# Differential attention and a gated recurrence on one core: heads unrolled, weighting in one fp32 product, factors of q on GpSimd

## The chip, the core and the metric

The program runs on one core of a Trainium2 chip. The time is the device time of one execution in microseconds; the median of three runs counts. The profile comes from a single execution recorded by the hardware profiler. TensorE is called PE there, its weight load PEld, VectorE is DVE, ScalarE is ACT, GpSimd is POOL and the queue of SyncE, which issues the DMAs, is SP. "PEclk" is the clock granted to TensorE as a share of 2.4 GHz; it has the two levels 0.50 (1.2 GHz) and 1.00.

## What is computed

One layer over 2048 tokens of width 1024, all in float32. One projection gives queries, keys and values of a differential attention (4 heads, two softmax maps of 64 features each, values of 128) and q, f, i and gate of a recurrence (HGRN2, 4 heads of 128). Both results go through one output projection, and a gated feed-forward part follows. What the change touches is this:

```python
# attention, for each block of 128 queries; mask: key chunk <= query chunk (chunks of 64)
s = jnp.einsum('bhqd,bhkd->bhqk', q_blk, k)
p = jax.nn.softmax(jnp.where(mask, s, -jnp.inf), axis=-1).reshape(B, H, 2, Q_BLOCK, S)
w = p[:, :, 0] - lam * p[:, :, 1]
out = jnp.einsum('bhqk,bhkv->bhqv', w, v)          # then RMS norm per head
# recurrence: S_t = diag(f_t) S_{t-1} + k_t v_t^T,  o_t = S_t^T q_t,  k_t = 1 - f_t
# then orr = rms_norm(o) * silu(gate)
```

## The kernel before

The program has three stages, one after the other, each a block of five engine programs that meet by semaphores: `project`, `mix_tokens` and `feed`. TensorE multiplies in fp32r. Where full precision is wanted, an operand is split into a high part in fp32r and the low rest, and three products (high x high, high x low, low x high) are added up.

`project` goes through 4 blocks of 512 tokens in 14 units of 256 columns. Of the units V (4 and 5) ScalarE writes the high part (L329) and VectorE the low part (L410); both are stored to `v_hi` and `v_lo` (L208).

`mix_tokens` runs a hardware loop over the 4 heads (`Fori`), on each engine (L778, L825, L889, L1022, L1140). Beside head h of attention it runs block h of the recurrence, all four of its heads at once. The body has 16 unrolled steps j, one for each block of 128 queries, and a seventeenth for what is left.

- A step scores both maps m against (j + 1) x 128 keys (`score`, L1066 to L1070) into a ring of four PSUM banks, in runs of up to two banks. VectorE takes the maximum of each run (`maximum`, L928, and over the runs L933). ScalarE takes the exponential and its sum (`exponentiate`, L851), which frees the banks. VectorE then forms inverse sums and the difference of both maps in one pass over the keys (`combine`, L948 to L957).
- One step later the weights are turned by TensorE in groups of four tiles (`turn`, L1081) into one of two PSUM banks. ScalarE writes their high part (`group_high`, L861), VectorE the low part (`group_low`, L963), and TensorE multiplies three times per tile with v (`weigh`, L1093 to L1095). There are 136 tiles per head. ScalarE reads the output and its squares (`read_output`, L866 and L870).
- The recurrence is spread over the steps as "fills", two in each of the first 15 steps, through one PSUM bank `fill_bank`: four diagonals (L1107), 14 level products (7 levels x 2 sides, L1117), four transposes of k, then output and state by turns (L1131 to L1136). A fill may start when the one before it has been read. After the fill of a level, VectorE multiplies q with a factor (`raise_level`, L970; at the diagonals L985) and only then copies the fill under a mask (L992). GpSimd meanwhile multiplies k (L839). The next level of that side waits for both. GpSimd also forms the factors (L832) and multiplies the output with the gate (L844).
- At the end of a head, outside the steps, come square roots, reciprocals and 16 scalings (L1051) of the output, then eight chunks of four transposes each (L1178) with a copy by ScalarE (L916, L918) and the stores of `mix`. Before the loop turns, SP has issued the loads of k, v and q for the next head (L793 to L807); k and v have a single buffer.

`feed` does the output projection and the feed-forward part. All its products have 512 columns.

Of the kernel before, what the change touches and what calls it, by code (L numbers as in the profile page):

```python
# [16 lines left out]
P = 128  # L17
D = 1024
SEQ = 2048
# [100 lines left out]
def project(nc, x, attn_g, w_in, q_g, k_g, ident, pair_sel, eps, out, masks):  # L120
# [15 lines left out]
    with ExitStack() as ctx:  # L136
# [66 lines left out]
        def destinations(u, tok):  # L203
# [3 lines left out]
            if u in V:  # L207
                return [token_dst(out[k], V[0], u, tok) for k in ("v_hi", "v_lo")]  # L208
# [65 lines left out]
        HANDED = [(u, t) for u in (*V, *HQ, *HG) for t in range(UT)]  # L274
# [6 lines left out]
        def _(act):  # L281
# [24 lines left out]
            def finish(i, n):  # L306
# [20 lines left out]
                for t in range(UT):  # L327
                    if u in V:
                        nc.scalar.activation(first[:, t, :].bitcast(F32R), banks[t][:], ACT.Copy).then_inc(act_part, 1)  # L329
                    elif u in HQ or u in HG:  # L330
                        nc.scalar.activation(second[:, t, :], banks[t][:], ACT.Sigmoid).then_inc(act_part, 1)
                    elif u in HI:
# [4 lines left out]
                if u in HI or u in HF:  # L337
                    last.then_inc(finished[par].sem, 1)
# [23 lines left out]
        def _(dve):  # L362
# [20 lines left out]
            def finish(i, n):  # L383
# [140 lines left out]
def mix_tokens(nc, mid, lambdas, subln_g, hgrn_g, ident, eps, mask, mix):  # L524

# [36 lines left out]
    GATE_STEP = len(FILLS) // 2  # L562
    assert HEADS == BLOCKS and GATE_STEP < SEQ // P
    STEPS = SEQ // P
    RING = 4
    RUN_BANKS = 2
    GROUP = 512 // P
    MASKED = -1e30

    def banks_of(j):  # L570

        return j // GROUP + 1
# [3 lines left out]
    for j in range(STEPS):  # L576
        for m in range(2):
            runs[j, m], key, left = [], 0, (j + 1) * P
            while left:
                n = min(RING - at, RUN_BANKS, -(-left // 512))  # L580
                width = min(left, n * 512)
                runs[j, m].append((at, key, width))
                at, key, left = (at + n) % RING, key + width, left - width
    assert at == 0
    order = [(j, m, r) for j in range(STEPS) for m in range(2) for r in range(len(runs[j, m]))]
    RUNS = len(order)
    MAX_RUNS = max(len(rs) for rs in runs.values())
    RUN_AT = {key: n for n, key in enumerate(order)}

    freed, last_in = {}, {}  # L590
    for n, (j, m, r) in enumerate(order):
        bank, _, width = runs[j, m][r]
        mine = range(bank, bank + -(-width // 512))
        freed[j, m, r] = max([last_in.get(x, -1) for x in mine]) + 1
        last_in.update({x: n for x in mine})
    GROUPS = sum(banks_of(j) for j in range(STEPS))
    GROUP_AT = {(j, g): sum(banks_of(i) for i in range(j)) + g for j in range(STEPS) for g in range(banks_of(j))}
    assert GROUPS % 2 == 0

    def tiles_in(j, g):  # L600

        return min(GROUP, j + 1 - g * GROUP)

    with ExitStack() as ctx:
        a = Alloc(nc, ctx, "att")


        q_hl = [a.sb(f"q_hl{b}", [P, 2, TB], F32R) for b in range(2)]
        q_lh = [a.sb(f"q_lh{b}", [P, 2, TB], F32R) for b in range(2)]
        k_hl = a.sb("k_hl", [P, 2, SEQ], F32R)  # L610
        v_hi = a.sb("v_hi", [P, STEPS, P], F32R)
        v_lo = a.sb("v_lo", [P, STEPS, P], F32R)
# [14 lines left out]
        wt_hi = [a.sb(f"wt_hi{b}", [P, 512], F32R) for b in range(2)]  # L627
        wt_lo = [a.sb(f"wt_lo{b}", [P, 512], F32R) for b in range(2)]
        o_all = a.sb("o_all", [P, STEPS, P])
# [4 lines left out]
        o_turned = a.sb("o_turned", [P, SEQ])  # L634
# [7 lines left out]

# [10 lines left out]
        ro_turned = r.sb("o_turned", [P, HEADS, TB])  # L653
        fill_bank = r.bank("fill")

        waited = a.sem("waited")
# [4 lines left out]
        k_in = [a.sem(f"k_in{b}") for b in range(2)]  # L661
# [10 lines left out]
        group_turned = a.sem("group_turned")  # L672
        group_hi = a.sem("group_hi")
        group_lo = a.sem("group_lo")
# [6 lines left out]
        o_turn_done = a.sem("o_turn_done")  # L681
        o_staged = a.sem("o_staged")
# [991 lines left out]
```

## Time and profile before

| | us |
|---|---|
| median of 3 runs | 3421.8 |
| lowest, highest | 3421.25, 3426.63 |
| span of the profiled execution | 3422.3 |
| TensorE busy | 3191.2 (93%) |
| VectorE busy | 1561.6 (46%) |
| ScalarE busy | 1158.8 (34%) |
| GpSimd busy | 143.5 (4%) |

The busy times are sums over the whole span. The ends of matmuls are modelled and each overlaps the next one, so a product's cost is read from the distance between two starts. The three stages lie at about 0 to 749, 749 to 1691 and 1691 to 3422 us.

### The profile page before, as it was taken

To read this page: it belongs to the slowest core of one execution; us is meant where nothing else is said; L and a number is where in the kernel's file an instruction comes from. 1 tells how busy PE (TensorE), PEld (TensorE's weight loads), DVE (VectorE), ACT (ScalarE), POOL (GpSimd) and SP (SyncE) were. 2 spreads that over 40 slices of the span, in tenths; PEclk is the share of its full clock that TensorE was granted. 3 is DMA by queue.
4 is the path that set the end of the run, shared out by engine and by line. 5 is a ranking of instruction groups with operands and counts; after the bars stand their busy time and mean duration, and the time that the engine had idled before them with its cause. 6 is when DMAs were issued, how large, how long until landed. Compare 5 with 4: busy or idle time off the path is not lost.

```text
span 3422.3 us, 44330 instructions
## 1 busy us (share of the span) xinstructions
PE 3191.2 (93%) x16832; PEld 2767.6 (81%) x16832; DVE 1561.6 (46%) x2066; ACT 1158.8 (34%) x1713; POOL 143.5 (4%) x122
## 2 busy tenths in 40 slices
PE   6999999979878888888699999999999999999999
PEld 5898989868778778777588887888878888788887
DVE  3434243426747657667435533355333543334432
ACT  3333333322523424424333322333223332233322
POOL 3000000002011101110000000000000000000000
PEclk9999999986957858769699999999999999999999
DMA  3545454554141231321632234323342333433334
GB/s 126 170 151 181 141 169 143 189 173 113 26 123 38 66 108 38 87 65 35 191 103 91 95 111 130 97 94 98 105 135 93 98 98 102 136 95 98 98 98 129
DMA packets 337554, 379.45 MB, mean 111 GB/s; under 512 B 11760, under 2 KB 286704, under 8 KB 337392
## 3 DMA queue, kind: packets, MB, share of 16 engines
q1 hardware_dynamic: 337392, 377.14, 35.6%
q8 instruction: 120, 1.97, 0.2%
q14 instruction: 42, 0.34, 0.0%
HBM read 314.19 MB, written 62.91 MB: 110 GB/s over the span
## 4 chain that ended last, share of the span: by engine, by line
PE 47%; DMA 1%; issue 1%; ACT 1%; SPq 0%; DVE 0%; DVEq 0%; ACTq 0%
PE feed_prod L1514 15%; PE feed_prod L1516 15%; PE feed_prod L1515 15%; DMA feed_gate_work<-mix 1%; PE feed_prod L1577 1%; PE feed_sums L1530 1%; PE feed_turned L1543 0%; ACT feed_ff_hi L1381 0%; DMA feed_w_raw<-in_w_out_dram 0%; SPq L1305 0%; ACT feed_ff_work L1281 0%; SPq L1293 0%; PE feed_scales L1591 0%; SPq L1269 0%; DVE feed_ff_lo L1443 0%
## 5 line engine op out<-in xcount | busy, mean ns | idle before, releaser
L1514 PE MATMUL feed_prod<-feed_h_hi,feed_w_hi 128*128 128x512 f32 x1408 | 548.9, 390 | 0.0
L1516 PE MATMUL feed_prod<-feed_h_hi,feed_w_lo 128*128 128x512 f32 x1408 | 547.8, 389 | 0.0
L1515 PE MATMUL feed_prod<-feed_h_lo,feed_w_hi 128*128 128x512 f32 x1408 | 547.8, 389 | 0.0
L1438 DVE TENSOR_TENSOR feed_w_lo<-feed_w_raw,feed_w_hi 128x2048 fp32r<-128x2048 f32 (+1 forms) x152 | 339.6, 2234 | 383.7 <-ACT feed_w_hi L1373 383.7
L1514 PE MATMUL feed_prod<-feed_ff_hi,feed_w_hi 128*128 128x512 f32 x960 | 381.6, 398 | 32.3 <-DVE feed_ff_lo L1443 22.4
L1373 ACT ACTIVATE feed_w_hi<-feed_w_raw 128x2048 fp32r<-128x2048 f32 (+1 forms) x152 | 283.4, 1865 | 356.6 <-PE feed_prod L1516 317.6
L1515 PE MATMUL feed_prod<-feed_ff_lo,feed_w_hi 128*128 128x512 f32 x960 | 377.1, 393 | 0.0
L1516 PE MATMUL feed_prod<-feed_ff_hi,feed_w_lo 128*128 128x512 f32 x960 | 376.9, 393 | 0.0
L851 ACT ACTIVATE att_expo<-att_ring,att_neg_max 128x1024 f32<-128x1024 f32 (+4 forms) x192 | 165.2, 864 | 434.7 <-DVE att_neg_max L928 234.7
L1516 PEld LDWEIGHTS feed_prod<-feed_h_hi,feed_w_lo 128*128 128x128 f32 x1408 | 264.3, 188 | 55.2
L1515 PEld LDWEIGHTS feed_prod<-feed_h_lo,feed_w_hi 128*128 128x128 f32 x1408 | 264.4, 188 | 54.8
L1514 PEld LDWEIGHTS feed_prod<-feed_h_hi,feed_w_hi 128*128 128x128 f32 x1408 | 264.4, 188 | 54.0
L1514 PEld LDWEIGHTS feed_prod<-feed_ff_hi,feed_w_hi 128*128 128x128 f32 x960 | 182.6, 190 | 69.9 <-DVE feed_ff_lo L1443 22.6
L506 PE MATMUL proj_prod<-proj_w_hi,proj_h_hi 128*128 128x256 f32 x768 | 219.3, 286 | 0.0
L367 DVE TENSOR_TENSOR proj_w_lo<-proj_w_raw,proj_w_hi 128x2048 fp32r<-128x2048 f32 x57 | 130.5, 2290 | 190.3 <-ACT proj_w_hi L288 190.3
L507 PE MATMUL proj_prod<-proj_w_lo,proj_h_hi 128*128 128x256 f32 x768 | 217.2, 283 | 0.0
L508 PE MATMUL proj_prod<-proj_w_hi,proj_h_lo 128*128 128x256 f32 x768 | 217.2, 283 | 0.0
L1516 PEld LDWEIGHTS feed_prod<-feed_ff_hi,feed_w_lo 128*128 128x128 f32 x960 | 182.3, 190 | 38.5
L1515 PEld LDWEIGHTS feed_prod<-feed_ff_lo,feed_w_hi 128*128 128x128 f32 x960 | 182.8, 190 | 36.7
L516 PE MATMUL proj_prod<-proj_h_hi,proj_w_hi 128*128 128x512 f32 x512 | 204.4, 399 | 7.7 <-DVE proj_w_lo L367 5.9
L1093 PE MATMUL att_out<-att_v_hi,att_wt_hi 128*128 128x128 f32 x544 | 183.3, 337 | 25.6 <-DVE att_wt_lo L963 24.7
L518 PE MATMUL proj_prod<-proj_h_hi,proj_w_lo 128*128 128x512 f32 x512 | 200.6, 392 | 0.0
(171 smaller groups left out, 5310.7 us busy)
## 6 DMA issues: line engine op xcount, KB each, us to landing
proj_w_raw<-in_w_in_dram SPq DMA_DIRECT2D x58, 1024.0 KB, 7.1
feed_w_raw<-in_w_gate_dram SPq DMA_DIRECT2D x44, 1024.0 KB, 5.4
feed_w_raw<-in_w_up_dram SPq DMA_DIRECT2D x44, 1024.0 KB, 5.4
feed_w_raw<-in_w_down_dram SPq DMA_DIRECT2D x32, 1024.0 KB, 5.9
feed_w_raw<-in_w_out_dram SPq DMA_DIRECT2D x18, 1024.0 KB, 6.7
feed_w_raw<-in_w_down_dram SPq DMA_DIRECT2D x16, 768.0 KB, 4.5
proj_x_tok<-in_x_dram SPq DMA_DIRECT2D x5, 2048.0 KB, 12.8
feed_x_piece<-in_x_dram SPq DMA_DIRECT2D x17, 512.0 KB, 4.2
```

The costliest lines, as they stand in the source:

```text
L506: pe.matmul(dst, hi[:, s, tok], wh[:, s, :], start=s == 0, stop=False)
L507: pe.matmul(dst, hi[:, s, tok], wl[:, s, :], start=False, stop=False)
L508: last = pe.matmul(dst, lo[:, s, tok], wh[:, s, :], start=False, stop=s == KS - 1)
L516: pe.matmul(dst, wh[:, s, col], hi[:, s, :], start=s == 0, stop=False)
L518: last = pe.matmul(dst, wl[:, s, col], hi[:, s, :], start=False, stop=s == KS - 1)
L851: nc.scalar.activation(expo[j % 2][:, m, key:key + width], ring[:, bank * 512:bank * 512 + width], ACT.Exp, bias=neg_max[:, j % 2, m:m + 1 ...
L1093: pe.matmul(out_bank[:, 0:P], hi, v_hi[:, kt, :], start=kt == 0, stop=False)
L1373: nc.scalar.activation(w_hi[slot][:, 0:slabs, :], w_raw[slot][:, 0:slabs, :], ACT.Copy).then_inc(w_hi_made, 1)
L1438: nc.vector.tensor_tensor(w_lo[slot][:, 0:slabs, :], w_raw[slot][:, 0:slabs, :], w_hi[slot][:, 0:slabs, :].bitcast(F32), ALU.subtract).the ...
L1514: pe.matmul(dst, w_hi[slot][:, k, col], hi[:, s, :], start=first, stop=False)
L1515: pe.matmul(dst, w_hi[slot][:, k, col], lo[:, s, :], start=False, stop=False)
L1516: return pe.matmul(dst, w_lo[slot][:, k, col], hi[:, s, :], start=False, stop=stop)
```

## The change

The hardware loop over the heads is gone. All engines run through one sequence of 64 steps s (and two more), so that a step may hold score work of one head and turning, weighting and reading of the head before. Buffers that a head had alone are doubled: the first 512 keys (`k_first`), `v` and `o_all`.

v stays one fp32 array. ScalarE copies the turned weights in fp32 into one of four buffers (`take_group`), and `weigh` makes one fp32 product per tile. `group_low` goes. The weighting of groups 2 and 3 of a step moves behind the first scores of the step after the next.

GpSimd now multiplies q as well, right behind k on each side and level, and at the diagonals. VectorE keeps the masked copy. The two sums of `combine` become one instruction. VectorE's order in a step is the first maximum, then `combine` of the step before.

The end of a head moves into the next one: roots in its step 1, scaling (`normalise`, one instruction for 16) in step 2, and two chunks in each of steps 3 to 6 through three staging buffers, each stored when it is made. The last head's end stays behind its last step. SP's order of loads and stores changes with it.

Core of the diff:

```diff
-                return [token_dst(out[k], V[0], u, tok) for k in ("v_hi", "v_lo")]
+                return [token_dst(out["v"], V[0], u, tok)]
...
-                    if u in V:
-                        nc.scalar.activation(first[:, t, :].bitcast(F32R), banks[t][:], ACT.Copy).then_inc(act_part, 1)
-                    elif u in HQ or u in HG:
+                    if u in HQ or u in HG:
                         nc.scalar.activation(second[:, t, :], banks[t][:], ACT.Sigmoid).then_inc(act_part, 1)
...
-                elif u in V:
-                    for t in range(UT):
-                        dve.wait_ge(act_part, handed(i, n, t))
-                        last = nc.vector.tensor_tensor(second[:, t, :].bitcast(F32R), banks[t][:], first[:, t, :], ALU.subtract)
...
+    def chunks_at(s):
+        h, j = divmod(s, STEPS)
+        if s == TOTAL + 1:
+            return [(HEADS - 1, c) for c in range(CHUNKS)]
+        first = 2 * (j - FIRST_CHUNK_STEP)
+        if 0 < h < HEADS and 0 <= first < CHUNKS:
+            return [(h - 1, first), (h - 1, first + 1)]
+        return []
...
-        wt_lo = [a.sb(f"wt_lo{b}", [P, 512], F32R) for b in range(2)]
-        o_all = a.sb("o_all", [P, STEPS, P])
+        wt = [a.sb(f"wt{b}", [P, 512]) for b in range(WT)]
+        o_all = [a.sb(f"o_all{b}", [P, STEPS, P]) for b in range(2)]
...
+            def store(h, c):
+                n = h * CHUNKS + c
+                sp.wait_ge(staged, n + 1)
+                if c < TURNS:
+                    dst = mix[h * P:(h + 1) * P, c * 512:(c + 1) * 512]
+                else:
+                    dst = mix[W + (c - TURNS) * P:W + (c - TURNS + 1) * P, h * TB:(h + 1) * TB]
+                sp.dma_start(dst, stage[n % STAGES][:]).then_inc(stored[n % STAGES], 16)
...
+                    if h:
+                        step_scored(h - 1, STEPS - 1)
+                    load_first_k(h + 1)
+                    if h:
+                        sp.wait_ge(group_used, WEIGH[h * STEPS - 1, groups_of(h * STEPS - 1) - 1] + 1)
+                    load_v(h + 1)
+                    sp.wait_ge(q_ready[1], h * UPDATES + 2)
+                    load_features(rf, "hf", h + 1, rf_in)
                 step_scored(h, GROUP - 1)
                 load_q(h, 2)
+                if h:
+                    for c in range(CHUNKS):
+                        store(h - 1, c)
+                    sp.wait_ge(r_gated, h)
...
+                    sp.wait_ge(fill_done, filled(h, fill_at("k", 1, CH - 1)))
+                    load_features(rk, "hk", h + 1, rqk_in)
+                    step_scored(h, 3 * GROUP - 1)
+                    load_q(h + 1, 0)
+                    sp.wait_ge(fill_done, filled(h, len(FILLS) - 1))
+                    load_features(rq, "hq", h + 1, rqk_in)
+                    load_tokens(rv, "hv", h + 1, rv_in)
+                    step_scored(h, STEPS - 1)
+                    load_rest_k(h + 1)
...
+                for side in range(2):
+                    pool.wait_ge(fill_done, filled(h, fill_at("diagonal", side, HALF - 1)))
+                    nc.gpsimd.tensor_tensor(half(rq, side), half(rq, side), half(rf, side), ALU.mult).then_inc(q_ready[side], 1)
...
-                fill_read.wait(pool, filled(h, len(FILLS) - 1))
+                        pool.wait_ge(q_ready[side], h * UPDATES + m + 1)
+                        nc.gpsimd.tensor_tensor(runs_of(rq, side, m, 1), runs_of(rq, side, m, 1), factor(side, m, 1), ALU.mult).then_inc(q_ready[side], 1)
...
+            def take_group(s, g):
+                k, n = WEIGH[s, g], tiles_in(s, g) * P
+                slot = SLOT["w", s, g]
+                act.wait_ge(slot_turned, slot + 1)
+                if k >= WT:
+                    act.wait_ge(group_used, k - WT + 1)
+                nc.scalar.activation(wt[k % WT][:, 0:n], turned[slot % 2][:, 0:n], ACT.Copy).then_inc(slot_taken, 1)
+            def take_chunk(h, c):
+                slot, n = SLOT["f", h, c], h * CHUNKS + c
+                act.wait_ge(slot_turned, slot + 1)
+                if n >= STAGES:
+                    act.wait_ge(stored[n % STAGES], 16 * (n // STAGES))
+                col = g_col if c < TURNS else rg_col
+                nc.scalar.activation(stage[n % STAGES][:], turned[slot % 2][:], ACT.Copy, scale=col[:]).then_inc(slot_taken, 1)
+                act.wait_ge(slot_taken, slot + 1)
+                act.sem_inc(staged, 1)
...
+            for s in range(TOTAL + 2):
+                h, j = divmod(s, STEPS)
+                live = s < TOTAL
+                groups = range(groups_of(s - 1)) if 1 <= s <= TOTAL else ()
+                if live:
+                    exponentiate(s, 0)
+                if s >= 2 and groups_of(s - 2) > 2:
+                    read_output(s - 2)
+                if j == 1 and h:
+                    take_roots(h - 1)
+                if live and j < FILL_STEPS:
+                    read_fill(h, 2 * j)
+                for g in groups[:2]:
+                    take_group(s - 1, g)
+                if live:
+                    exponentiate(s, 1)
+                    if j < FILL_STEPS:
                         read_fill(h, 2 * j + 1)
...
+                for g in groups[2:]:
+                    take_group(s - 1, g)
+                if 0 < len(groups) <= 2:
+                    read_output(s - 1)
+                for head, c in chunks_at(s):
+                    take_chunk(head, c)
...
-            def group_low(h, j, g):
-                k, n = GROUP_AT[j, g], tiles_in(j, g) * P
-                dve.wait_ge(group_hi, h * GROUPS + k + 1)
-                nc.vector.tensor_tensor(wt_lo[k % 2][:, 0:n], turned[k % 2][:, 0:n], wt_hi[k % 2][:, 0:n].bitcast(F32), ALU.subtract).then_inc(group_lo, 1)
...
-            def raise_level(h, side, m):
-                if m:
-                    dve.wait_ge(whole_made, h * LEVELS + m)
-                dve.wait_ge(q_ready[side], h * UPDATES + m + 1)
-                nc.vector.tensor_tensor(runs_of(rq, side, m, 1), runs_of(rq, side, m, 1), factor(side, m, 1), ALU.mult).then_inc(q_ready[side], 1)
...
+            def normalise(h):
+                dve.wait_ge(r_rms_made, h + 1)
+                nc.vector.reciprocal(ro_rrms[:], ro_rms[:]).then_inc(r_rrms_made, 1)
+                dve.wait_ge(o_rms_made, h + 1)
+                nc.vector.reciprocal(o_rrms[:], o_rms[:]).then_inc(o_rrms_made, 1)
+                dve.wait_ge(o_rrms_made, h + 1)
+                o = o_all[h % 2][:]
+                nc.vector.tensor_tensor(o, o, o_rrms[:].unsqueeze(2).to_broadcast([P, STEPS, P]), ALU.mult).then_inc(o_normed, 1)
+                dve.wait_ge(r_rrms_made, h + 1)
+                dve.wait_ge(r_gated, h + 1)
+                out = ro[:].rearrange("p c (h n) -> p (c h) n", n=C)
+                nc.vector.tensor_tensor(out, out, ro_rrms[:].unsqueeze(2).to_broadcast([P, CH * HEADS, C]), ALU.mult).then_inc(r_scaled, 1)
...
+            for s in range(TOTAL + 2):
+                h, j = divmod(s, STEPS)
+                live = s < TOTAL
+                fills = live and j < FILL_STEPS
+                if live:
+                    maximum(s, 0)
+                if 1 <= s <= TOTAL:
+                    combine(s - 1)
+                if fills:
+                    read_fill(h, 2 * j)
+                if live:
+                    maximum(s, 1)
+                if fills:
+                    read_fill(h, 2 * j + 1)
+                if live and h and j == FIRST_CHUNK_STEP - 1 or s == TOTAL + 1:
+                    normalise(h - 1)
...
+            def weigh(s, g):
+                h, j = divmod(s, STEPS)
+                pe.wait_ge(slot_taken, SLOT["w", s, g] + 1)
+                if g == 0 and s:
+                    pe.wait_ge(o_read, s)
+                    pe.wait_ge(o_squared, s)
+                for t in range(tiles_in(s, g)):
...
-                    hi, lo = wt_hi[k % 2][:, t * P:(t + 1) * P], wt_lo[k % 2][:, t * P:(t + 1) * P]
-                    pe.matmul(out_bank[:, 0:P], hi, v_hi[:, kt, :], start=kt == 0, stop=False)
-                    pe.matmul(out_bank[:, 0:P], hi, v_lo[:, kt, :], start=False, stop=False)
-                    last = pe.matmul(out_bank[:, 0:P], lo, v_hi[:, kt, :], start=False, stop=kt == j)
+                    last = pe.matmul(out_bank[:, 0:P], wt[WEIGH[s, g] % WT][:, t * P:(t + 1) * P], v[h % 2][:, kt, :], start=kt == 0, stop=kt == j)
...
+            def turn_chunk(h, c):
+                slot = SLOT["f", h, c]
+                if c < TURNS:
+                    pe.wait_ge(o_normed, h + 1)
+                else:
+                    pe.wait_ge(r_scaled, h + 1)
+                open_slot(slot)
+                for t in range(GROUP):
+                    src = o_all[h % 2][:, c * GROUP + t, :] if c < TURNS else ro[:, t, (c - TURNS) * C:(c - TURNS + 1) * C]
+                    last = pe.transpose(turned[slot % 2][:, t * P:(t + 1) * P], src, ident[:])
+                last.then_inc(slot_turned, 1)
...
+                    score(s, 0)
+                if s >= 2:
+                    for g in range(2, groups_of(s - 2)):
+                        weigh(s - 2, g)
+                if fills:
+                    if j == 0:
+                        pe.wait_ge(rqk_in, 32 * (h + 1))
+                    fill(h, 2 * j)
+                if live:
+                    score(s, 1)
+                for g in groups[:2]:
+                    turn(s - 1, g)
+                if fills:
+                    fill(h, 2 * j + 1)
+                if j == 1 and live:
+                    pe.wait_ge(v_in[h % 2], 16 * (h // 2 + 1))
+                for g in groups:
+                    if g < 2:
+                        weigh(s - 1, g)
+                    if g + 2 in groups:
+                        turn(s - 1, g + 2)
+                for head, c in chunks_at(s):
+                    turn_chunk(head, c)
```

## Rows read from the trace of the kernel before

**Rows 1.** Stages and low-clock stretches: us, busy (instructions), PEclk, DMA share, GB/s.
```profile
761.00:1691.00 930.00, 784.84 (x4544) 711.81 (x4544) 587.51 (x1035) 353.64 (x833) 110.40 (x88) 0.75 0.29 79
1720.00:3422.00 1702.00, 1681.70 (x7705) 1400.37 (x7703) 681.53 (x683) 529.53 (x523) 0.00 (x0) 0.99 0.34 106
949.00:993.00 44.00, 36.50 (x157) 33.15 (x157) 19.72 (x39) 16.48 (x33) 3.21 (x6) 0.50 0.47 110
997.00:1062.00 65.00, 55.64 (x236) 51.70 (x236) 35.46 (x61) 12.77 (x40) 9.51 (x7) 0.50 0.22 72
```

**Rows 2.** The same view, pieces of 3 us at the second head's end.
```profile
1178.00:1181.00 3.00, 1.12 (x6) 0.68 (x4) 3.00 (x1) 0.00 (x0) 2.92 (x2) 1.00 0.16 53
...
1193.00:1196.00 3.00, 3.00 (x17) 3.00 (x16) 0.11 (x1) 0.77 (x3) 0.00 (x0) 0.50 0.99 231
```

**Rows 3.** Timeline of weight loads: start us, us, engine, line, out<-in, count.
```profile
937.83 0.97 PEld L1136 LDWEIGHTS rec_fill<-rec_v,rec_k_tok 128*128 128x128 f32 x8 [0.88 <-ACT rec_o L885]
...
939.70 0.19 PEld L1093 LDWEIGHTS att_out<-att_v_hi,att_wt_hi 128*128 128x128 f32 x1
939.82 0.19 PEld L1094 LDWEIGHTS att_out<-att_v_lo,att_wt_hi 128*128 128x128 f32 x1
...
963.36 0.33 PEld L1093 LDWEIGHTS att_out<-att_v_hi,att_wt_hi 128*128 128x128 f32 x1
963.57 0.33 PEld L1094 LDWEIGHTS att_out<-att_v_lo,att_wt_hi 128*128 128x128 f32 x1
...
1004.99 1.78 PEld L1107 LDWEIGHTS rec_fill<-rec_q,rec_k 128*128 128x128 f32 x8 [0.56 <-DVE rec_score L981]
```

**Rows 4.** Groups of TensorE: busy us, mean ns, idle before.
```profile
L1094 PEld LDWEIGHTS att_out<-att_v_lo,att_wt_hi 128*128 128x128 f32 x544 | 133.1, 245 | 0.0
...
L1136 PE MATMUL rec_fill<-rec_v,rec_k_tok 128*128 128x128 f32 x128 | 18.5, 288 | 10.7 <-ACT rec_o L885 10.7
```

**Rows 5.** Timeline across the first head's end, TensorE.
```profile
984.53 0.41 PE L1095 MATMUL att_out<-att_v_hi,att_wt_lo 128*128 128x128 f32 x1
...
1001.38 0.47 PE L1066 MATMUL att_ring<-att_k_hl,att_q_hl 128*128 128x128 f32 x1 [6.69 <-issue]
```

**Rows 6.** Waits, attention stage: in total, times, longest us.
```profile
ACT att_expo L851 <- DVE att_neg_max L928: 234.7, 63, 8.6
...
PE att_out L1093 <- DVE att_wt_lo L963: 24.7, 32, 2.1
PE rec_fill L1117 <- DVE rec_score L992: 23.9, 20, 2.7
PE att_ring L1066 <- ACT att_expo L851: 23.3, 23, 2.6
```

**Rows 7.** Groups by shape of VectorE and GpSimd: busy us, mean ns.
```profile
L970 DVE TENSOR_TENSOR rec_q<-rec_q,rec_whole 128x512 f32<-128x512 f32 x48 | 74.0, 1541 | 56.5 <-PE rec_fill L1117 55.2 <-issue 0.9
L957 DVE SCALAR_TENSOR_TENSOR att_expo<-att_expo,att_ratio 128x1920 f32<-128x1920 f32 x4 | 13.9, 3476 | 0.1
L957 DVE SCALAR_TENSOR_TENSOR att_expo<-att_expo,att_ratio 128x2048 f32<-128x2048 f32 x4 | 9.4, 2352 | 0.1
...
L839 POOL TENSOR_TENSOR rec_k<-rec_k,rec_whole 128x512 f32<-128x512 f32 x48 | 53.8, 1122 | 210.0 <-PE rec_fill L1117 210.0
L844 POOL TENSOR_TENSOR rec_o<-rec_o,rec_gate 128x2048 f32<-128x2048 f32 x4 | 18.3, 4577 | 318.8 <-DVE rec_state L997 318.8
```

**Rows 8.** DMA issues: count, KB each, median us to landing.
```profile
mix<-att_o_turned SPq DMA_DIRECT2D x16, 256.0 KB, 6.3
```

**Rows 9.** Timeline of step 14 and the next step's start.
```profile
929.80 0.45 PE L1066 MATMUL att_ring<-att_k_hl,att_q_hl 128*128 128x512 f32 x1
...
931.34 2.21 DVE L928 TENSOR_REDUCE att_run_neg_max<-att_ring 128x1 f32<-128x1024 f32 x2
...
933.78 1.11 ACT L851 ACTIVATE att_expo<-att_ring,att_neg_max 128x1024 f32<-128x1024 f32 x1 [5.38 <-DVE att_neg_max L933]
...
944.87 0.45 PE L1066 MATMUL att_ring<-att_k_hl,att_q_hl 128*128 128x512 f32 x1
```

More of the change, by code:

```diff
@@ L591, in mix_tokens @@
[L591 to L602, printed above, removed]
+    RUN_AT = {}
@@ new lines, in mix_tokens @@
+    for s in range(TOTAL):
+        for m in range(2):
+            for r in range(len(runs[s, m])):
+                RUN_AT[s, m, r] = len(RUN_AT)
+    freed, last_in = {}, {}
+    for (s, m, r), n in RUN_AT.items():
+        bank, _, width = runs[s, m][r]
+        mine = range(bank, bank + -(-width // 512))
+        freed[s, m, r] = max([last_in.get(x, -1) for x in mine]) + 1
+        last_in.update({x: n for x in mine})
+    MAX_RUNS = max(len(rs) for rs in runs.values())
+    assert all(len(runs[s, 0]) == len(runs[s, 1]) for s in range(TOTAL))
@@ new lines, in runs_through, with partial_runs @@
+    def runs_through(s, m):
+        return RUN_AT[s, m, len(runs[s, m]) - 1] + 1
+    def partial_runs(s, m):
+        return sum(len(runs[key]) for key in runs if key <= (s, m) and len(runs[key]) > 1)
+    def chunks_at(s):
[6 more added lines that the diff above has]
+        return []
@@ new lines, in load_rest_k, with load_v, load_features @@
+            def load_rest_k(h):
+                for part, name in ((low, "qk_hi"), (high, "qk_lo")):
+                    sp.dma_start(k_rest[part].bitcast(F32), rows(name, h, W, slice(TB, SEQ))).then_inc(k_rest_in, 16)
+            def load_v(h):
+                src = mid["v"][:, h * P:(h + 1) * P].rearrange("(t p) n -> p t n", p=P)
+                sp.dma_start(v[h % 2][:], src).then_inc(v_in[h % 2], 16)
+            def load_features(tile, name, b, sem):
+                sp.dma_start(tile[:], mid[name][:, b * TB:(b + 1) * TB].rearrange("(h p) n -> p h n", p=P)).then_inc(sem, 16)
@@ new lines, in _ @@
+            load_rest_k(0)
+            load_q(0, 1)
+            load_tokens(rv, "hv", 0, rv_in)
+            load_tokens(rgate, "hgate", 0, rgate_in)
+            for h in range(HEADS):
+                last = h == HEADS - 1
+                if not last:
+                    if h:
[6 more added lines that the diff above has]
+                    load_features(rf, "hf", h + 1, rf_in)
@@ L823, in _ @@
+            for c in range(CHUNKS):
+                store(HEADS - 1, c)
+            for b in range(STAGES):
+                sp.wait_ge(stored[b], 16 * len(range(b, HEADS * CHUNKS, STAGES)))
         @block.gpsimd
         def _(pool):
-            with pool.Fori(0, HEADS) as h:
-                pool.wait_ge(r_in, h * (16 * R_DMAS) + 16 * R_DMAS)
+            for h in range(HEADS):
+                pool.wait_ge(rf_in, 16 * (h + 1))
                 for m in range(LEVELS):
```

425 lines of the change are left out of this document (141 added, 284 removed).

## The prediction

> **What bounds the kernel now.** I first read the kernel by its three stages. The middle one, attention with its recurrence, takes 930 us of 3422; the stage after it holds TensorE busy 1682 of 1702 us at the full clock, and the change does not touch it [rows 1]. In the middle stage TensorE is busy 785 us (84%), VectorE 588, ScalarE 354 and GpSimd 110, and the granted clock is 0.75 [rows 1]. So TensorE bounds this stage too, but at a clock that is only at times the full one.
>
> Next I cut one head, 1002 to 1233 us, into 3 us pieces. TensorE is at 1.2 GHz (0.50) for the first 60 us, at 2.4 GHz in the middle, and at 1.2 GHz again over the head's end; [rows 1] has both low stretches for the turn from the first to the second head. The fall at the end comes right behind a piece in which TensorE is busy 1.12 of 3 us. Then it stays low for 40 us though a piece such as 1193 to 1196 is full to the brim [rows 2]. That piece holds little but products of 128 columns.
>
> Then I looked at pitches, from start to start, because a matmul's duration in the trace overlaps the next one. In the weighting of the values (L1093 to L1095) one fp32r product of 128 columns follows the other in 0.21 us at the low clock and in 0.11 us at the full one [rows 3]. An fp32 product shows as two records: 64 products of L1136 stand as 128 [rows 4]. The weight loads give the pitch of these records: eight of L1107 span 1.78 us at the low clock, less one of 0.33 over seven steps, 0.207 us; eight of L1136 span 0.97 at the full clock, less 0.19, 0.111 us [rows 3]. So one fp32 record costs the same pitch as one fp32r product.
>
> Last come the waits and the head's end. From the last weighting (984.53) to the next head's first score (1001.38) lie 16.8 us, of which 6.69 stand under "issue", at the jump back of the loop [rows 5]. Inside the head TensorE waits for VectorE's low part (L963), for L992 and for the exponentials L851 [rows 6].
>
> **The change part by part.**
>
> *One fp32 product for three fp32r ones.* 544 tiles give up three pitches and take two. Which clock they see follows from the mean weight load of L1094, 245 ns [rows 4]: with 0.19 us at the full clock and 0.33 at the low one [rows 3], 38% run low. The mean pitch is 0.62 x 0.111 + 0.38 x 0.213 = 0.150 us, and 544 x 0.150 = 81 us of TensorE's path go. The nearest rows for the new cost are L1131 and L1136, which are fp32 with 128 columns as well; the whole 1.78 us of L1107 over eight instead of seven pitches give 0.222 [rows 3], 0.009 more for 1088 records, which would leave 71 us, the lower bound; the upper one is 81, since no row has a cheaper record.
>
> The Trainium skill says in "FP8 and Floating Point Precision" (TensorE Precision Notes) that true fp32 makes 4 passes through the array. If a pass cost what an fp32r product costs here, the change would add a pitch per tile and lose 81 us where I book a gain. The trace shows two records at one pitch each, so I give that outcome a small chance as a rival below.
>
> *The low part on VectorE goes* (L963). VectorE has slack, so the time itself is worth nothing; the wait of TensorE for it, 24.7 us [rows 6], goes. What is late next is ScalarE's copy, which stood ahead of L963 anyway. The weighting of groups 2 and 3 moves one step later with four weight buffers, which covers this copy too.
>
> *q's factors move to GpSimd.* The 48 L970 of levels 1 to 6 take 74 us from VectorE [rows 7]; eight of level 0 and eight wide L985 I put at a quarter of that, 20. On GpSimd the 48 cost what k's do, 1.12 us [rows 7], 54, and the sixteen others at most two of these each, 36: GpSimd comes to 110 + 90 = 200 of 930 us, no bound. On VectorE they stood between a fill and its copy L992, and TensorE's single fill bank waits for that copy: 23.9 us [rows 6]. An L970 of 1.54 us goes from a chain of about 2.5, so I book 60%, 14 us. New is a serial chain on GpSimd: k, then q, 2.3 us per side and level, before the next level of that side. What hides it is the step between them, 10 us and more; without that cover it costs 56 x 2.3 us. GpSimd's work also slows VectorE's: the 1920-wide L957, which falls beside L844 in three heads of four, took 3.48 us on average against 2.35 for one of 2048 [rows 7], half of itself more. The L957 of steps 2 to 8 are short, some 7 us per head together by their widths, so this costs between 0 and 4 x 3.5 = 14 us; I take 0, because VectorE is not the bound there.
>
> The Trainium skill's "GPSIMD Engine Reference" (4.1 Engine selection) would keep an elementwise product of tensors on VectorE, since GpSimd takes about twice as long. It speaks against this part. The rows have k's on GpSimd at 1.12 us and q's on VectorE at 1.54, when both run at once.
>
> *Heads unrolled and spread ends.* The 16.8 us hold 32 transposes of 0.213 us, 6.8 us, which stay but go into steps 3 to 6 of the next head. The other 10 us, three times, go: 30 us [rows 5]. The code without a loop has no jump back; the trace shows "issue" waits of this kind only at the returns. I take 0 for fetching straight code, with one 6.69 us wait per head, 27 us, as the upper bound. Behind SP's waits for stores stand the loads of q 3 and k; their consumers are four steps away. The last head still ends alone, now through three staging buffers for eight chunks. A store lands in 6.3 us [rows 8] and two rounds wait for it, partly behind the work: 8 us lost, between 0 and 13.
>
> *v in one array* takes 16 VectorE operations and half the stores from the first stage, which TensorE bounds: 0.
>
> *The clock.* The fall at 1181 comes behind a wait for VectorE's L957, slowed by GpSimd, with the turns and the weighting behind it. In the new order the next score and the deferred weighting lie in between, so I expect the stretch to stay at the full clock. From 949 to 993 TensorE is busy 36.5 us at the low clock [rows 1]; less 31 tiles x 0.213 = 6.6 already booked, half of the remaining 30 us is 15, of which I book 14 per head: 56. A short dip of 10 us per head (near 881 and 1113) is worth some 3 us: 12. The low start of a head, 65 us [rows 1], should end about one step sooner, since less work of 128 columns stands in it: 5 per head, 20. Less 4 for tiles counted low in the first part. Sum 84; bounds 0 and about 165 (the start of each head warm too: 55.6 us busy, half of it 28, less what is booked).
>
> **The sum.** 81 + 25 + 14 + 30 + 84 - 8 = 226 us. Against the profiled run's span of 3422.3, which lies 0.5 us over the median of 3421.8, that gives 3196. A second way: step 14 now takes from 929.80 to 944.87 [rows 9]. Its chain afterwards is twice (one score pair 0.93, two maxima 2.21, 0.15 for the smaller, an exponential of 1.11 and 0.2 for its sum) = 9.2 us [rows 9] plus some 1.8 for state and fill, so 11 in place of 15. Six such steps at 3.5, step 15 with its weighting (40 us, to 984.53) down to some 23, and the first eight steps with 36 tiles x 0.213 and a quarter of the fill bank's 14 are 49 us per head; four of these, the 30 of the head ends and the 20 of the sooner full clock are 246, less 8 for the end: 238, or 3184. I forecast between the two: **3190 us**.
>
> **The rivals.**
>
> *A: the clock stays as it is now.* For it: TensorE full of 128-column work stayed low from 1193 to 1196 [rows 2]. Then only 81 + 25 + 14 + 30 - 8 = 142 us go: 3280. Chance 0.22.
>
> *B: TensorE is warm nearly throughout.* For it: the falls come behind waits, the stage after it, with hardly a wait, stays at the full clock for 1702 us [rows 1], and the new order takes most waits away. Then all 165 of the clock: 3115, and with shorter waits some 3095. Chance 0.18.
>
> *C: an fp32 product costs four pitches.* 544 x 0.150 more instead of less: 3190 + 163 = 3353. Against it stand the two records of L1136 [rows 4]. Chance 0.02.
>
> *D, slower than before: GpSimd's chain becomes the bound.* In steps 2 to 8 of each head four of its operations stand in a row per step. At 1.12 us each they take 4.5 us against steps of 10 to 14. If each cost what the contended L844 does, 4.58 us [rows 7], a step would take 18.3 + 3 us, about 11.7 more, in 28 steps: 3190 + 328 = 3518. It decides from about 4.1 us more per fill, that is, over 3 us per operation, where L839 has 1.12 [rows 7]. Chance 0.03.
>
> *E: the change doesn't do what it says.* A load or a code fetch that comes late leaves the heads unjoined: 30 + 27 us back, 3247. Chance 0.06.
>
> **How the numbers follow.** The forecast has 0.49. A lies at the upper side and B at the lower, so the range for 8 in 10 reaches from 3090 to 3290. A change under 0.2% (7 us) could not be told from none. Only C and D lie far off, and only D is slower: faster 0.95, same 0.01, slower 0.04.
>
> **What the new profile would show.** Two records per tile at 0.11 or 0.21 us in the weighting; VectorE some 200 us less busy in the stage and GpSimd at about 190; no "issue" wait of 6.7 us between heads; scores of a new head among the weighting of the last; granted clock of the stage over 0.80. The stage should last about 700 us. It would be wrong if TensorE waited for rec_q on GpSimd, if the clock stayed at 0.75 or less, or if ScalarE's exponentials, which now wait 235 us for VectorE's maxima [rows 6], became a chain that leaves TensorE idle for long.

## The result: 3134.5 us, 290 us less than before

| | before | after |
|---|---|---|
| median of the runs | 3424.2 us | 3134.5 us |
| span of the profiled execution | 3422.3 us | 3133.0 us |
| mean granted clock of TensorE | 0.925 | 0.979 |

The ratio is 0.915, with a 95% interval of 0.913 to 0.917. The before of this table has one run more than the three shown ahead, which puts its median 2.4 us higher. The gain is 290 us; the forecast had 232. The range (3090 to 3290) holds the time, but the time lies nearer to rival B (20 us away) than to the forecast (56 us).

### The profile page after: what moved, and what is told of

Same layout as the page of the kernel before. It is cut to its first block, busy times and chain, and to the rows that moved or that the text cites. A ratio compares the mean times of both kernels' runs of the same rounds, so it can differ in the third digit from the quotient of the medians.

```text
span 3133.0 us, 40790 instructions
## 1 busy us (share of the span) xinstructions
PE 2956.9 (94%) x16288; PEld 2561.2 (82%) x16288; DVE 1381.6 (44%) x1702; ACT 1156.5 (37%) x1712; POOL 248.7 (8%) x186
## 4 chain that ended last, share of the span: by engine, by line
PE 52%; DMA 1%; issue 1%; ACT 1%; SPq 0%; DVE 0%; DVEq 0%; ACTq 0%
PE feed_prod L1476 17%; PE feed_prod L1478 16%; PE feed_prod L1477 16%; DMA feed_gate_work<-mix 1%; PE feed_prod L1539 1%; PE feed_sums L1492 1%; PE feed_turned L1505 0%; ACT feed_ff_hi L1343 0%; DMA feed_w_raw<-in_w_out_dram 0%; SPq L1267 0%; ACT feed_ff_work L1243 0%; SPq L1255 0%; PE feed_scales L1553 0%; SPq L1231 0%; DVE feed_w_lo L1412 0%
## 5 line engine op out<-in xcount | busy, mean ns | idle before, releaser
L511 PE MATMUL proj_prod<-proj_h_lo,proj_w_hi 128*128 128x512 f32 x512 | 200.0, 391 | 0.0
```

What stands on the lines that cost most here:

```text
L511: pe.matmul(dst, wh[:, s, col], lo[:, s, :], start=False, stop=False)
```

## The profile after

First the page's busy times, then the windows view (us; busy and instructions of PE, PEld, DVE, ACT, POOL; PEclk; DMA share; GB/s) of the time from attention's first score to TensorE's end, of before and after, and of the attention stage after:

```profile
PE 2956.9 (94%) x16288; PEld 2561.2 (82%) x16288; DVE 1381.6 (44%) x1702; ACT 1156.5 (37%) x1712; POOL 248.7 (8%) x186
```
```profile
761.10:3418.00 2656.90, 2482.66 (x12320) 2125.66 (x12319) 1278.22 (x1724) 893.55 (x1366) 110.40 (x88) 0.91 0.32 97
```
```profile
762.40:3129.00 2366.60, 2248.34 (x11776) 1919.25 (x11775) 1108.30 (x1376) 891.88 (x1365) 215.66 (x152) 0.98 0.34 102
762.40:1410.00 647.60, 550.82 (x4000) 505.78 (x3999) 419.70 (x688) 355.54 (x835) 215.66 (x152) 0.93 0.35 93
935.00:949.00 14.00, 9.54 (x43) 8.95 (x43) 7.43 (x10) 4.19 (x10) 6.25 (x4) 0.51 0.64 175
```

Before and after differ by 544 TensorE records, one per tile. The attention stage lasts 648 us at a clock of 0.93, where [rows 1] has 930 us at 0.75. In each of heads 1 to 3 one wide stretch is left at the low clock, for instance 935 to 949, and one dip of 3.4 us. The first head still starts low, until 781, and the last one ends low.

The gain can be split by a bookkeeping that adds up by its making. From the first score to the end, the time is TensorE's idle time, plus its busy time; and its busy time is counted as its work at the full clock plus half of what it was busy at the low clock. It says how large each part is, not what caused it. All runs of this study are split in the same way here, each from its one profiled execution (us, worked out from TensorE's records merged and the stretches of the granted clock; the last column is the median of the timed runs; an execution that is profiled can lie some us off it, up to 7 here):

| kernel | time to the end | idle | busy at low clock | work at full clock | median |
|---|---|---|---|---|---|
| before | 2656.8 | 174.1 | 408.2 | 2278.6 | 3424 |
| + fp32 product alone | 2538.9 | 192.3 | 242.1 | 2225.5 | 3303.8 |
| + loop written out alone | 2630.8 | 155.5 | 391.5 | 2279.6 | 3398.0 |
| + q's factors on GpSimd alone | 2605.7 | 156.1 | 343.8 | 2277.7 | 3367.4 |
| + these three | 2432.7 | 146.9 | 120.5 | 2225.5 | 3197.2 |
| after (the change) | 2366.2 | 117.9 | 68.1 | 2214.3 | 3134.5 |
| after, q's factors on VectorE | 2445.2 | 129.6 | 202.3 | 2214.4 | 3206.7 |
| after, two fp32r products | 2374.6 | 117.6 | 92.2 | 2210.8 | 3143.2 |
| after, three fp32r products | 2413.9 | 102.1 | 86.7 | 2268.5 | 3189.0 |
| after, one fp32r product | 2332.2 | 125.8 | 104.9 | 2154.0 | 3101.2 |
| after, no deferral | 2408.3 | 141.8 | 94.0 | 2219.5 | 3177.4 |
| after, scalings in pieces | 2367.7 | 114.4 | 77.4 | 2214.6 | 3136.9 |
| after, scalings on ScalarE | 2340.8 | 106.0 | 40.0 | 2214.8 | 3109.4 |
| the same, last head on VectorE | 2333.7 | 98.6 | 40.1 | 2215.0 | 3100.7 |

Before to after: 64.3 us less work, 56.2 us less idle time, and (408.2 - 68.1) / 2 = 170.0 us less lost to the clock. Together 290.5, and the measured time to the end differs by 290.6. So 59% of the gain is clock by this count.

What TensorE still waits for, in the stretch of attention (in total, times, longest, us):

```profile
PE att_turned L1040 <- DVE att_expo L935: 28.6, 15, 6.1
PE att_ring L1023 <- ACT att_expo L831: 26.2, 24, 2.3
...
PE rec_fill L1084 <- DVE rec_score L950: 6.1, 12, 0.8
...
PE att_turned L1063 <- DVE att_o_all L971: 5.3, 1, 5.3
PE att_out L1051 <- ACT att_wt L840: 4.2, 9, 0.8
```

The waits of [rows 6] for the low part are gone, that for the fill bank's reader fell from 23.9 to 6.1 us, and there is no "issue" between heads. New at the top is the weighted exponential (L935): 28.6 us, where it had 8.7 before (the row of L957 under the first experiment). Its longest waits, of up to 6.1 us, are in step 3 of heads 1 to 3. Counted from one first score to the next, that step lasts 7.2 us in head 0, but 17.6, 17.4 and 17.6 us in the others. Here is that step (start, duration, engine, line; the waits of TensorE in brackets):

```profile
930.51 2.29 DVE L971 TENSOR_TENSOR att_o_all<-att_o_all,att_o_rrms 128x2048 f32<-128x2048 f32 x1
930.53 3.62 POOL L819 TENSOR_TENSOR rec_q<-rec_q,rec_f 128x512 f32<-128x512 f32 x1
...
932.72 3.58 DVE L975 TENSOR_TENSOR rec_o<-rec_o,rec_o_rrms 128x2048 f32<-128x2048 f32 x1
934.11 3.33 POOL L817 TENSOR_TENSOR rec_k<-rec_k,rec_whole 128x512 f32<-128x512 f32 x1
...
937.41 1.28 POOL L819 TENSOR_TENSOR rec_q<-rec_q,rec_whole 128x512 f32<-128x512 f32 x1
937.49 1.61 DVE L935 SCALAR_TENSOR_TENSOR att_expo<-att_expo,att_ratio 128x384 f32<-128x384 f32 x1
...
939.16 0.90 PE L1040 MATMUL att_turned<-all_ident,att_expo 128*128 128x128 f32 x3 [6.13 <-DVE att_expo L935]
```

The two scalings of the last head's outputs (L971, L975) stand on VectorE ahead of the sum that TensorE waits for. They and GpSimd's products take turns: each operation ends about its own time after the other engine's has ended. L971 ends at 932.80; L819, which begins beside it, ends 1.35 us later and counts 3.62 us. L975 ends at 936.30, 2.15 us behind that. L817 ends 1.14 us behind L975. At the last head's end, with nothing of GpSimd's beside it, L975 takes 2.29 us.

## The experiments

**The fp32 product alone**

```
-    hi, lo = wt_hi[..], wt_lo[..]
-    pe.matmul(out_bank, hi, v_hi); pe.matmul(out_bank, hi, v_lo); pe.matmul(out_bank, lo, v_hi)
+    pe.matmul(out_bank, wt[..], v[..])        # kernel before; v in one array, L963 gone
```

> The kernel before with the fp32 product alone: one fp32 product per tile, v in one array, the weights in one copy, no low part on VectorE. Theory 1 (the clock follows the waits): 81 us of pitches and the 25 us wait for L963 go, the head ends and the fill bank's waits stay, so the granted clock of the middle stage stays near 0.75 to 0.80: about 3315 us, with at most 30 us of clock more, 3285. Theory 2 (the fp32 products themselves hold TensorE's clock up): the clock of the stage rises above 0.90 with this edit alone, and the time falls to some 3200 us.

3303.8 us, ratio 0.965 (0.962 to 0.968): 120 us. The time lies inside theory 1's range, but not for its reasons. The work falls by 53 us, which is the product. The clock gives back 83. Theory 1 allowed some 50: its 30, and the 21 of its 81 us that are pitches at the low clock. The stage's clock is 0.83 (761 to 1581), between the two theories. And the idle time rises by 18 us, though the 24.7 us for L963 are gone. The waits of before (first row) and of this kernel show where most of them went:

```profile
PE att_turned L1081 <- DVE att_expo L957: 8.7, 4, 2.6
```
```profile
PE rec_fill L1097 <- DVE rec_score L979: 36.0, 37, 2.7
...
PE att_turned L1064 <- DVE att_expo L948: 22.4, 17, 4.0
...
PE att_out L1075 <- ACT att_wt L852: 9.5, 12, 1.8
```

L979 is the copy out of the fill bank, which had 23.9 us [rows 6], and L948 the weighted exponential. Most of the wait moved to the next operations of VectorE. The rest went to ScalarE's copy of the weights (L852), which TensorE did not wait for before.

**The loop over heads written out**

```
-            with pe.Fori(0, HEADS) as h:      # and on the four other engines
+            for h in range(HEADS):
```

> The kernel before with the loop over heads written out on all five engines, nothing else. If the 6.69 us of issue between heads are the jump back, three of them go and nothing else changes: 3422 - 20 = 3402 us. If they are a fetch of code that straight code also needs, the time stays within 5 us of 3422. If the short pause is what lets the clock fall, more than 60 us go.

3398.0 us, ratio 0.992 (0.989 to 0.994): 26 us. 18.6 are idle time, which is the three "issue" waits of before, and 8 are clock:

```profile
PE att_ring L1066 <- issue: 18.6, 3, 6.7
```

The straight code of this run has no such wait between heads.

**q's factors on GpSimd alone, and back on VectorE in the changed kernel**

```
-            nc.vector.tensor_tensor(runs_of(rq, ..), runs_of(rq, ..), factor(..), ALU.mult)
+            nc.gpsimd.tensor_tensor(runs_of(rq, ..), runs_of(rq, ..), factor(..), ALU.mult)
```

> The kernel before with q's factors on GpSimd, nothing else. The prediction's step: 14 us go from the fill bank's wait: 3408 us. The rival: in the order of before there is no cover, and GpSimd slows VectorE's sums as L844 slowed L957 (3.48 against 2.35 us), so it stays within 10 us of 3422 or is slower by up to 30 us.

> The changed kernel with q's factors back on VectorE, nothing else. By the prediction's step 14 us come back: 3148 us. If VectorE has become what a step waits for in the new order (90 us of ScalarE's waits lie behind its maxima), up to 94 us of its work come back on the path and the clock dips more often: 3180 to 3230 us. If the contention of GpSimd and VectorE in the long step (18.3 us) costs as much as the work saves, the time stays at 3134 us.

The first takes 57 us away (3367.4; ratio 0.981, 0.976 to 0.986), the second gives 72 back (3206.7; ratio to before 0.936, 0.933 to 0.939). The first one's four runs spread widely, from 3341.3 to 3377.0 us. In the profiled executions the two edits make 51 and 79 us. Of these the idle time is 18.0 and 11.7 us, close to the 14 that were booked. Nearly all of the rest is clock: 32 us in the first and 67 in the second. In the second, the wait for the fill bank's reader is 25.2 us instead of 6.1, and the clock falls behind a pause in step 3 (windows view):

```profile
PE rec_fill L1086 <- DVE rec_score L952: 25.2, 25, 1.4
```
```profile
953.00:956.00 3.00, 0.57 (x3) 0.34 (x3) 3.00 (x4) 0.38 (x1) 0.73 (x1) 0.82 0.00 0
956.00:959.00 3.00, 3.00 (x15) 3.00 (x15) 0.14 (x1) 0.67 (x2) 0.00 (x0) 0.50 0.00 0
```

It stays at 1.2 GHz until about 975. The changed kernel has a pause there too, but its low stretch ends at 948.7 after 13.6 us. With VectorE's queue ahead of each fill, heads 1 to 3 have five or six low stretches each; without it they have two.

**Do the fp32 products hold the clock up?**

```
-    pe.matmul(out_bank[:, 0:P], wt[..], v[..], ..)
+    for n in range(2): pe.matmul(out_bank[:, 0:P], wt[..], v[..], ..)   # v and wt as fp32r; 3 and 1 too
```

> The changed kernel with two fp32r products per tile in place of one fp32 product, which shows as two records; v and the weights are rounded to fp32r and the low parts are left out, so the weighted sum has only the high part (twice). TensorE has as many records of 128 columns as in the changed kernel. Theory 1 (the clock follows the waits): same time, 3134 us, within 10. Theory 2 (the fp32 products hold the clock up): the clock of the middle stage falls towards 0.75 to 0.85 and the time rises by 60 to 150 us.

> The changed kernel with three fp32r products per tile, TensorE's work of the kernel before, but no low part on VectorE (left out of the sum, the high part three times). If TensorE bounds the steps and the clock stays full: 544 x 0.111 = 60 us more, 3194 us. If the extra work drops into waits (ScalarE and VectorE bound the early steps) less, 3160. If the clock falls with more work of 128 columns: 3215 us (81 us) or more.

> The changed kernel with one fp32r product per tile (half of the product's TensorE work, the low parts left out). If TensorE bounds the steps: 60 us less, 3074 us. If the chain score, maximum, exponential is the bound of the steps, the time stays near 3134 us, and the clock falls because TensorE has less to do: 3120 us or above.

Not in the changed kernel. These three kernels leave the low parts of v and of the weights out of the sum; only their times count. With two fp32r products the time is 3143.2 us (ratio 0.918, 0.915 to 0.921, which overlaps that of the change), the clock 0.974. That is 12 us of clock lost and 4 of work won, not the 60 to 150 us of theory 2. In the order of before this was not tried. So whether the 83 us of clock of the first experiment came from the shorter product or from the waits that moved stays open. The third product costs 3189.0 - 3143.2 = 46 us (39 between the profiled runs: 58 of work, which is 0.106 us each, less 15 that fall into idle time and 3 of clock). One product instead of two saves 42 us, not 60: 57 of work, 8 of them turned into idle time and 6 lost to the clock. TensorE bounds the stage over most of its length: of the 57 us taken away, 8 came back as idle time.

**The three edits together**

> The kernel before with the three edits of the first runs together (fp32 product, loop over heads written out, q's factors on GpSimd) and the order of the steps of before: each head still ends alone, and each step weighs what it turned. Alone they brought 120, 26 and 57 us. If they add up: 3424 - 203 = 3221 us, and the new order of the steps is worth the other 87 of the 290 us. If each one makes the next one's clock better: 3170 us or below, and the order is worth less than 50. If they share one gain (the same low stretches): 3260 us, and the order is worth 125.

3197.2 us, ratio 0.934 (0.931 to 0.936): 226 us, where the parts alone sum to 204. In the profiled runs the three together bring 29 us more than the parts' sum: 20 of clock and 9 of idle time. All that the change has beyond the three edits is worth the other 63: the new order of the steps, the deferral, the spread ends, and the small edits to `combine`. In the profiled runs it is 66: 29 idle, 26 clock, 11 of work (why the records are 11 us shorter stays open; their ends are modelled).

**No deferral**

```
-    for g in groups:
-        if g < 2: weigh(s - 1, g)             # groups 2 and 3 one step later
+    for g in groups: weigh(s - 1, g)
```

> The changed kernel with groups 2 and 3 of a step weighed in the same step as groups 0 and 1, nothing else. If the deferral hides ScalarE's copy of the weights: 28 steps have such groups (7 of each head's 16, steps 8 to 15 less one), and each would wait about the 1.5 us of a copy behind its turns, 40 to 60 us more with some clock lost, 3180 us. If the copies are long done when TensorE comes to them: 3134 us, within 6.

3177.4 us, ratio 0.928 (0.926 to 0.929): the deferral is worth 43 us, two thirds of those 63. The time is the 3180 that was expected if the deferral hid ScalarE's copy of the weights, but that is luck: the wait for the copy (`att_wt`) is 5.1 us, where the change has 4.2. What comes back is the wait for the exponentials:

```profile
PE att_ring L1023 <- ACT att_expo L831: 45.0, 32, 2.8
```

It was 26.2. A likely reading, not tested further, is that TensorE comes to the next score earlier, with less work between, while ScalarE has yet to read the bank that the score writes to.

**Step 3 of heads 1 to 3**

```
-    nc.vector.tensor_tensor(o, o, o_rrms[..].to_broadcast([P, STEPS, P]), ALU.mult)   # step 2
+    nc.vector.tensor_tensor(o[:, part], o[:, part], ..)                 # a: pieces in steps 2 to 5
+    nc.scalar.activation(o[:, t], o[:, t], ACT.Copy, scale=o_rrms[:, t:t + 1])        # b: ScalarE
```

> The changed kernel with the two scalings at a head's end cut into a piece for each chunk and spread over steps 2 to 5 of the next head. Step 3 of heads 1 to 3 lasts 18.3, 17.7 and 18.4 us now, against 6.6 in head 0, and the clock falls from 935.1 to 948.7 us. If the two long VectorE instructions (2.29 and 3.58 us) ahead of the sum that TensorE waits for make it, step 3 falls to 9 to 11 us and some dips vanish: 3 x 8 = 24 us less, 3110 us. If the many small instructions cost as much: 3134 us, within 6.

> The changed kernel with the scalings at a head's end on ScalarE, one 128x128 piece at a time by the scale of its copy, spread over steps 2 to 5, in place of two long instructions on VectorE (2.29 and 3.58 us, then GpSimd's 3.62 and 3.33 us beside them, against 1.15 and 1.28 apart from them). If it is the meeting of VectorE and GpSimd that makes step 3 of heads 1 to 3 last 18 us, it falls to about 9 and no other step takes the time over: 3 x 9 = 27 us less, 3107 us. If ScalarE's 8 x 0.37 us per step hold up its exponentials as much: 3134 us or up to 20 more.

The pieces on VectorE change nothing: 3136.9 us. Step 3 falls to 14.4 us in head 1, but step 5, where pieces of the second scaling meet GpSimd, rises from 8.0 to 12.9. On ScalarE the time falls to 3109.4 us (ratio 0.908, 0.906 to 0.909), 25 us under the change (12 of idle time and 14 of clock in the profiled executions). Step 3 lasts 8.1 us and head 1 has no low stretch at all:

```profile
931.23 1.50 POOL L819 TENSOR_TENSOR rec_q<-rec_q,rec_f 128x512 f32<-128x512 f32 x1
...
932.78 0.62 DVE L959 SCALAR_TENSOR_TENSOR att_expo<-att_expo,att_ratio 128x384 f32<-128x384 f32 x1
...
933.58 0.49 PE L1057 MATMUL att_turned<-all_ident,att_expo 128*128 128x128 f32 x3
```

L819 takes 1.50 us for 3.62, the weighted exponential 0.62 for 1.61, and TensorE turns 3.7 us after the step's first score, not 9.9.

```
+    if h == HEADS - 1: nc.vector.tensor_tensor(..)       # one piece per chunk; ScalarE for heads 0 to 2
```

> As the run before with the scalings on ScalarE for heads 0 to 2, but on VectorE, one piece per chunk, for the last head, where GpSimd has nothing beside it and ScalarE also has to copy the eight chunks. From the last output piece to the last chunk copy that run needs 19.6 us (1351.85 to 1371.41) where the changed kernel needs 13.7 (1384.08 to 1397.82). If the end of the last head sets when the next stage begins: 6 to 8 us less than 3109.4, 3102 us. If the loads of the next stage set it: 3109 us.

3100.7 us, ratio to before 0.905 (0.903 to 0.906): the fastest kernel of the study that computes the whole layer, 34 us under the change. From the last weighting to the next stage's first product now lie 25.9 us, against 34.5 with all scalings on ScalarE and 28.2 in the change.

## Why the prediction was right, and where its sizes were off

- *What bounds.* TensorE at a changing clock: right. The third product added costs most of its pitch, 46 of 58 us.
- *The product.* Two records per tile, x1088. 544 x 0.111 = 60 us of full-clock work against 53 for the product alone and 58 for the third fp32r product. The change has 64, of which 11 came with the rest of it. The other 21 of the 81 were low-clock pitches, so the split above counts them as clock; the clock terms were therefore 84 + 21 = 105 us. Rival C is out: the step of the fp32 product won 120 us where C would have lost. What fails is C's condition, that one of the four passes costs as much as an fp32r product. The Trainium skill's four passes of true fp32 ("FP8 and Floating Point Precision", TensorE Precision Notes) are not refuted by that, since the section gives no time for a pass. By the records here an fp32 product takes two fp32r pitches, 0.222 us at the full clock, so four passes would have some 0.055 us each (an estimate from that pitch and the page's four).

```profile
L1051 PEld LDWEIGHTS att_out<-att_v,att_wt 128*128 128x128 f32 x1088 | 136.0, 196 | 7.4 <-ACT att_wt L840 6.1 <-issue 0.7
```

A mean weight load of 196 ns against 245 [rows 4] says that hardly any of them ran at the low clock.

- *The idle terms.* 25 for L963, 14 for the fill bank, 30 for the head ends, less 8 at the end: 61 booked, 56 measured. The sum is right, its parts less so. The wait for L963 alone wasn't worth 25: most of it moved on. The last head's end was booked as 8 us lost, and it won 3.7: from the last weighting to the next stage 31.85 us before, 28.18 after. Step 3's new stall of some 3 x 10 us was not foreseen, and the shorter steps paid for it: step 14 lasts 11.1 us as the second way had it, and step 15 12.6 where that had 23. The turns and the weighting of step 15 fall into the next head's first two steps, which last 8.6 and 5.5 us.
- *The clock.* This is the term that was mis-sized: 105 booked, 170 measured. Where it lies shows when the column "busy at low clock" is laid out by the part of the head (us, all four heads; the clock costs half of it):

  | part | before | fp32 product alone | the three edits | after |
  |---|---|---|---|---|
  | steps 0 to 7 | 208 | 152 | 48 | 36 |
  | steps 8 to 12 (the dips) | 38 | 25 | 14 | 10 |
  | step 13 to the next first score | 144 | 43 | 42 | 4 |
  | the stage after | 20 | 23 | 18 | 19 |

  The heads' starts are what I had wrong. They gave back 86 us (half of 208 - 36), where I had booked 20 besides the products' share. I had put the low start down to work of 128 columns, but the same work runs at the full clock in the change, and most of the low time comes back (160 us busy) when nothing but q's factors return to VectorE. The runs point to the short waits among the fills; but the fp32 product alone, with more of these waits, also gained 28 us there, so they aren't the whole cause.

  The heads' ends and the dips gave back 70 and 14 us, near what was booked, but the reason that I gave for the ends holds for the smaller part only. I expected them to stay at the full clock because the new order puts a score and the deferred weighting in between. In the order of before the fp32 product alone already brought 51 of the 70 us, so that this term came out near its size is in part luck.

  In these terms the upper bound of 165 is 186 with the products' share, against 170 measured. It was the better guide, and B its rival: B's 3115 misses by 20 us, 16 of them clock, which the stall of step 3 holds down (moving it to ScalarE gives back 14).
- *q's factors.* 14 us of idle time: right to 4 us. Worth 57 to 72 in the medians, because of the clock. GpSimd comes to 216 us for the 200 booked:

```profile
L819 POOL TENSOR_TENSOR rec_q<-rec_q,rec_whole 128x512 f32<-128x512 f32 x48 | 61.1, 1274 | 0.0
...
L819 POOL TENSOR_TENSOR rec_q<-rec_q,rec_f 128x512 f32<-128x512 f32 x8 | 18.4, 2295 | 0.0
```

1.27 us for the 1.12 taken, and 2.3 us for the eight of level 0. No wait of TensorE's ends on GpSimd, so rival D is out. VectorE is busy 168 us less in the stage (587.5 to 419.7). The operations that left it had 188: 93 for L963 and 94 for q's factors.

- *GpSimd slows VectorE.* I took 0 of 0 to 14 us, since VectorE doesn't bound the short steps. In step 3 it does: the normalisation moved there, and it costs about the 25 us that the ScalarE variant wins. I had costed that move only for its transposes, though the scalings went along: every instruction of a moved step counts, and what it will meet there.

## What to carry to other kernels

Where TensorE's clock changes within a stage, split its time into idle, work and low-clock loss before and after. Here 12 to 18 us of idle time, taken away among the fills, were worth 57 to 72, because the clock came with them, and a wait removed alone mostly moved to the next operations of the same engine. A clock gain should be looked up where it lies: most of this one was there in the old order already. Long VectorE operations of two inputs and GpSimd's should not be put in the same place: cutting them did not help, giving them to ScalarE did, where ScalarE had room.

## What the runs showed of the hardware

- VectorE and GpSimd exclude each other for whole instructions of this kind: 3.62 us for a GpSimd product of 1.50, 3.58 for a VectorE one of 2.29, 1.61 for one of 0.62. Each ends behind the other engine's instruction by its own time less 0.1 to 0.2 us, and L971, which begins 0.02 us ahead of GpSimd's, is not slowed (2.29 us, as at the last head's end). The Trainium skill says so of VectorE instructions with two inputs from SBUF and a GpSimd one that reads it ("SBUF — State Buffer", SBUF: two separate sides): whichever starts first holds a shared port pair and "the other fully blocks". The trace agrees, with these numbers.
- One fp32 product of 128 columns takes as long as two fp32r ones: 3134.5 and 3143.2 us for 544 tiles of each, with 2214 and 2211 us of work at the full clock.
- The granted clock doesn't follow the total of idle time. 11.7 us more of it, in short waits among the recurrence's fills, cost 67 us of clock (q's factors back on VectorE); 23.9 us more, in waits of up to 2.8 us before a score of the later steps, cost 13 (no deferral). Both are from the profiled executions. What in the pattern decides stays open.
